# A two-block transformer kernel: the first block's output projection cut into two contraction halves, and the norm between the blocks done tile by tile

## What is computed

```python
sb_out = stick_breaking_attention(q, k, v)                  # 512 columns
sg_out = chunked_spatial_gating(u, vg, ...)                 # 512 columns
mixed = concatenate([rmsnorm(sb_out, sb_out_norm_g), rmsnorm(sg_out, sg_out_norm_g)])
h = h + mixed @ w_out
h = h + hierarchical_moe(rmsnorm(h, ffn_norm_g), ...)
x = rmsnorm(h, final_norm_g)                                # end of the first block
z = rms_norm(x, g_mix) @ w_in + b_in                        # start of the second block
```

## Time and profile before

| | us |
|---|---|
| median of three runs | 1077.96 (1077.39 to 1079.14) |
| profiled execution, time | 1080.09 |
| profiled execution, span | 1078.6 |
| PE busy in the span | 896.8 (83%) |
| DVE busy | 526.9 (49%) |
| ACT busy | 344.6 (32%) |
| POOL busy | 133.4 (12%) |

### The profile page before, as it was taken

How to read it: one execution, slowest core, us unless ns; L and a number is a source line. 1 busy time by engine, 2 the same in 40 slices (tenths; PEclk the granted TensorE clock), 3 DMA queues, 4 the chain that set the end, 5 groups by cost and what they waited for, 6 DMA issues and landing times.

```text
span 1078.6 us, 18062 instructions
## 1 busy us (share of the span) xinstructions
PE 896.8 (83%) x7891; PEld 724.1 (67%) x7891; DVE 526.9 (49%) x845; ACT 344.6 (32%) x463; POOL 133.4 (12%) x67
## 2 busy tenths in 40 slices
PE   8998988966475746475565899999999989999997
PEld 8987875533243424242342599689999989988986
DVE  4644554222131212112021769999997857635542
ACT  5624221100000001000000734557756446443531
POOL 1032400000000000000001288603210000000000
PEclk9998999888787868778688899999999999999999
DMA  9870748999999999999999645325568444546420
GB/s 343 260 300 2 300 168 371 426 426 427 426 428 428 428 428 430 428 428 430 428 428 420 198 162 191 117 93 171 168 211 283 173 170 166 207 157 218 173 78 39
DMA packets 86727, 299.98 MB, mean 278 GB/s; under 512 B 12381, under 2 KB 50701, under 8 KB 74253
## 3 DMA queue, kind: packets, MB, share of 16 engines
q1 hardware_dynamic: 86525, 299.13, 70.7%
q10 hardware_dynamic: 144, 0.00, 0.0%
HBM read 298.07 MB, written 1.05 MB: 277 GB/s over the span
## 4 chain that ended last, share of the span: by engine, by line
PE 52%; DMA 29%; DVE 14%; ACT 2%; issue 2%; SPq 1%; DVEq 0%
DMA mem<-in_w_up 25%; PE PS L1772 12%; PE PS L1773 12%; PE PS L1774 12%; PE PS L1954 8%; DVE PS L1547 6%; PE PS L1967 3%; DMA mem<-in_w_down 3%; DMA mem<-in_w_in 1%; DVE PS L1572 1%; PE PS L1940 1%; DMA mem<-in_w 1%; PE PS L1980 1%; PE PS L1746 1%; DVE PS L1568 1%
## 5 line engine op out<-in xcount | busy, mean ns | idle before, releaser
L1954 PE MATMUL PS<-mem 128*32 128x256 f32 x2048 | 156.6, 473 | 136.0 <-DMA mem<-in_w_up 135.4
L1954 PEld LDWEIGHTS PS<-mem 128*32 128x32 f32 x2048 | 83.6, 136 | 210.6 <-issue 184.6
L1774 PE MATMUL PS<-HT_hi,ring_rest 128*128 128x256 f32 x752 | 212.8, 283 | 0.0
L1774 PEld LDWEIGHTS PS<-HT_hi,ring_rest 128*128 128x128 f32 x752 | 143.9, 191 | 0.0
L1328 DVE TENSOR_TENSOR mem<-mem,PS 128x128 f32<-128x128 f32 x32 | 12.1, 379 | 261.2 <-ACT mem L809 261.2
L1772 PE MATMUL PS<-HT_hi,z_hi 128*128 128x256 f32 x440 | 124.9, 284 | 2.3 <-DVE ring_rest L1522 2.3
L1773 PE MATMUL PS<-HT_rest,z_hi 128*128 128x256 f32 x440 | 124.5, 283 | 0.0
L653 POOL TENSOR_TENSOR ring_rest<-mem,z_hi 128x2048 fp32r<-128x2048 f32 x19 | 87.6, 4622 | 95.1 <-DVE ring_rest L1522 55.9
L1685 DVE TENSOR_TENSOR ring_rest<-mem,mlp_hi 128x4096 fp32r<-128x4096 f32 x16 | 70.8, 4424 | 57.7 <-ACT mlp_hi L1027 57.7
L809 ACT ACTIVATE mem<-PS 128x128 f32<-128x128 f32 x32 | 8.9, 278 | 272.3 <-PE PS L1954 272.3
L1547 DVE SCALAR_TENSOR_TENSOR PS<-mem,CAW,PS 128x256 f32<-128x256 f32 x232 | 91.3, 480 | 0.0
(11 more groups left out here) (357 smaller groups left out, 1817.7 us busy)
## 6 DMA issues: line engine op xcount, KB each, us to landing
mem<-in_w_gate SPq DMA_DIRECT2D x32, 2048.0 KB, 16.5
mem<-in_w_up SPq DMA_DIRECT2D x32, 2048.0 KB, 20.9
mem<-in_w_down SPq DMA_DIRECT2D x31, 2048.0 KB, 12.7
mem<-in_w SPq DMA_DIRECT2D x16, 2048.0 KB, 8.1
mem<-in_w_in SPq DMA_DIRECT2D x30, 1024.0 KB, 5.3
mem<-in_w_in SPq DMA_DIRECT2D x4, 2048.0 KB, 18.3
mem<-in_w_b_out SPq DMA_DIRECT2D x4, 1536.0 KB, 8.9
mem<-in_w_out SPq DMA_DIRECT2D x2, 2048.0 KB, 14.7
```

What stands on the lines that cost most here:

```text
L1774: ins = nc.tensor.matmul(dst, s_rest, m_hi, start=False, stop=stop and n == len(terms) - 1, skip_group_check=True)
L1954: ins = nc.tensor.matmul(PS[SLOTS * j:SLOTS * (j + 1), bank, 0:2 * F_STRIP].rearrange("p (w n) -> p w n", w=2), xg[:, k, :], w[:, :, k, F_ ...
```

## The change

w_out is read so that a contraction chunk holds rows of one half only: chunks 0 to 3 the attention's 512 rows, 4 to 7 the gated unit's. The norm, turning, gain and split are then done for the gated half first, within the last pair of heads, and for the attention's half after it. The product is done in two halves of the contraction, the gated one first, summed in PSUM. The factor of both norms comes from Ln and Exp with one correcting step on DVE in place of a root. The tables are turned among the spatial weights. GpSimd splits w_out's second block first, into slot 3; the down load of expert 1 goes behind the product. Between the blocks, the work on a tile starts when its own two sums are in; GpSimd's first split waits for the normed rows; the first two products go pass by pass together; the first block's output rows go behind `rest_half(1)`.

The diff, its changed counts, index helpers and small loads left out:

```diff
-                   for n, at in enumerate((4 * SLOT_FLOATS, 4 * SLOT_FLOATS + HALF_FLOATS, a0 + D, a0 + D + HALF_FLOATS))]
+                   for n, at in enumerate((4 * SLOT_FLOATS, 4 * SLOT_FLOATS + HALF_FLOATS, 3 * SLOT_FLOATS, 3 * SLOT_FLOATS + HALF_FLOATS))]
...
+                    for half in range(2):
+                        ks = slice(KC // 2 * half, KC // 2 * (half + 1))
+                        sp.dma_start(chunked(n % RING, BLOCK)[:, ks, :], w_out1[half][:, :, b * BLOCK:(b + 1) * BLOCK]).then_inc(loaded[n % RING], 16)
...
-            sp.wait_ge(*in1_used(7))
-            load_down(1, *first[2])
             sp.wait_ge(rows, rows_before["ffn"])
...
             load_down(0, *second[2])
+            load_down(1, *first[2])
...
-            for n in range(4):
+            for n in OUT1_SPLIT:
                 raw, rest = out1_half(n)
-                if n == 2:
-                    pool.wait_ge(av_done, PAIRS)
-                    pool.wait_ge(hT_rest_ready, split_count("mix", 3))
...
             pool.wait_ge(z_hi_ready, 1)
+            pool.wait_ge(rows, rows_before["mix2"] + TT)
...
+            def mix_factor(col, rows_, *ready):
+                for tt in range(TT):
+                    act.wait_ge(*ready[tt])
+                    add_squares(rows_[tt], col + tt, square[:, 0:SB])
+                link(nc.scalar.activation(rstd[:, col:col + TT], ss[:, col:col + TT], ACT.Ln, scale=1.0 / SB, bias=eps[:, :]))
+                nc.scalar.activation(rstd[:, col:col + TT], rstd[:, col:col + TT], ACT.Exp, scale=-0.5).then_inc(rms_ready, 1)
...
             for pair in range(PAIRS):
                 if pair + 1 < PAIRS:
                     att_log(pair + 1)
+                else:
+                    mix_factor(6, [so[:, tt, :] for tt in range(TT)], (so_ready, 1), (so_ready, 2))
                 att_weights(pair)
-            act.preload_act_table_set(SQRT_SET)
...
+            split_hT("mix", range(TT))
+            mix_factor(4, [PS[:, 2 + tt, :] for tt in range(TT)], (av_done, PAIRS), (av_done, PAIRS))
+            split_hT("mix", range(TT, 2 * TT))
...
             gating(0)
+            gating(1)
             att_masked(2)
             att_softplus(3)
-            gating(1)
+            mix_rows("mix gated", 1, 6, [so[:, tt, :] for tt in range(TT)])
             att_masked(3)
...
+            apply_gain("mix", G_MIX, range(TT))
+            rest_hT("mix", range(TT))
+            mix_rows("mix", 0, 4, [PS[:, 2 + tt, :] for tt in range(TT)])
+            apply_gain("mix", G_MIX, range(TT, 2 * TT))
+            rest_hT("mix", range(TT, 2 * TT))
...
+            for tt in range(TT):
+                for n in (2 * tt, 2 * tt + 1):
+                    add_part(PACKS - 1, n)
+                    if n == 2:
+                        square_terms(0)
                 nc.vector.tensor_tensor(HG[:, tt, :], X[:, tt, :], g_first[:, :], ALU.mult).then_inc(gained, 1)
...
-            inverse_rms("first", 10, TT)
-            for tt in range(TT):
-                nc.vector.tensor_scalar(X[:, tt, :], HG[:, tt, :], rstd[:, 10 + tt:11 + tt], None, ALU.mult)
...
             rest_half(1)
+            inverse_rms("first", 10, TT)
+            for tt in range(TT):
+                nc.vector.tensor_scalar(X[:, tt, :], HG[:, tt, :], rstd[:, 10 + tt:11 + tt], None, ALU.mult)
             conv_a(0)
...
+            def out1_product(n, half):
+                pe.wait_ge(out1_rest_ready, OUT1_SPLIT.index(n) + 1)
+                for tt in range(TT):
+                    terms = rows_times(tt, out1_hi[n][:, :, :], out1_half(n)[1])[KC // 2 * half:KC // 2 * (half + 1)]
+                    ins = three_passes(out1_place(n, tt), terms, half == 1 and n % 2 == 0, half == 0)
...
+                if pair == PAIRS - 1:
+                    turn_mix(1, 0)
                 weighted_values(pair - 1)
             weighted_values(PAIRS - 1)
-            keep_busy(7, 4)
-            turn_rows("mix")
-            keep_busy(1, 3)
-            pe.wait_ge(hT_rest_ready, split_count("mix", 3))
...
+            pe.wait_ge(hT_rest_ready, split_count("mix", TT - 1))
+            out1_product(0, 1)
+            out1_product(1, 1)
+            turn_mix(0, TT)
+            out1_product(2, 1)
+            out1_product(3, 1)
+            pe.wait_ge(hT_rest_ready, split_count("mix", 2 * TT - 1))
             for n in range(4):
+                out1_product(n, 0)
...
+            def first_pair(hi, rest):
...
-                        if isinstance(r, int) and (r, h, i) == (0, 0, 0):
-                            first_times_hT(PS[:, 0, 0:T], hi, rest, slice(0, P), "mix2", z_rest_ready, 1).then_inc(z_ps, 1)
+                        if isinstance(r, int) and (r, h) == (0, 0):
+                            if i == 1:
+                                first_pair(hi, rest)
```

More of the change, by code:

```diff
@@ L296, in build @@
         norms = ["attn", "mix", "ffn", "mix2", "mlp2"]
-        rms_ready, rms_order = sem("rms_ready"), ("attn", "vg", "mix", "ffn", "mix2", "mix2 second", "first", "mlp2", "last")
+        rms_ready, rms_order = sem("rms_ready"), ("attn", "vg", "mix gated", "mix", "ffn", "mix2", "mix2 second", "first", "mlp2", "last")
         rows, rows_before = sem("rows"), {"attn": 0, "mix": TT, "ffn": 3 * TT, "mix2": 4 * TT, "mlp2": 5 * TT}
@@ L417, in late_used, with out1_count, out1_place @@
             return (f_ps, 16 * half + 4 * (b + 1)) if b < 4 else (w2_used, 4 * half + b - 3)
-        def pre_count(n):
-            return 16 * (n // RING + 1)
+        def out1_count(n):
+            return 16 * (n // RING + 2)
+        MIX_QUARTERS = [(tt, slice(KC // 2 * half, KC // 2 * (half + 1))) for half in (1, 0) for tt in range(TT)]
+        OUT1_SPLIT = (2, 3, 0, 1)
+        def out1_place(n, tt):
+            return PS[:, (0 if n < 2 else 6) + tt, (n % 2) * HALF:(n % 2 + 1) * HALF]
         def in1_used(n):
@@ L712, in split_hT @@
                 for n in quarters:
-                    tt, ks = n // 2, slice(4 * (n % 2), 4 * (n % 2) + 4)
+                    tt, ks = MIX_QUARTERS[n] if name == "mix" else (n // 2, slice(4 * (n % 2), 4 * (n % 2) + 4))
                     act.wait_ge(hT_ready, hT_count(name, n))
@@ L1498, in _, with square_terms @@
             collect(e + PACK - 1, PACK - 1)
-            add_pack(PACKS - 1)
-            for tt in range(TT):
+            def square_terms(tt):
                 dve.wait_ge(first_squares, tt + 1)
@@ L1885, in _, with turn_mix @@
             spatial_mixing(0)
+            def turn_mix(half, n0):
+                for tt in range(TT):
+                    pe.wait_ge(rows, TT + n0 + tt + 1)
+                    if n0 > 0:
+                        pe.wait_ge(hT_ready, hT_count("mix", n0 - TT + tt))
+                    for k in range(KC // 2):
+                        ins = nc.tensor.transpose(PS[:, 4 + tt, k * P:(k + 1) * P], HN[:, tt, KC // 2 * half + k, :], ident[:, :])
+                    ins.then_inc(turned, 1)
+            def out1_product(n, half):
+                pe.wait_ge(out1_rest_ready, OUT1_SPLIT.index(n) + 1)
+                for tt in range(TT):
+                    terms = rows_times(tt, out1_hi[n][:, :, :], out1_half(n)[1])[KC // 2 * half:KC // 2 * (half + 1)]
+                    ins = three_passes(out1_place(n, tt), terms, half == 1 and n % 2 == 0, half == 0)
+                    if half == 0:
+                        ins.then_inc(out1_ps, 1)
             for pair in range(1, PAIRS):
```

121 lines of the change are left out of this document (67 added, 54 removed).

## The result

The changed kernel took 1069.65 us in the median (1068.80 to 1071.34) against 1077.81, a ratio of 0.9924 (95%: 0.9907 to 0.9941). The forecast was 1069.7 us. The profiled execution took 1071.34 us, 1069.6 of it span; that of before was 1078.6. The total was right.

The account below looks back on a forecast made before the run. The prediction took the path through attention and projection to the weight stream's restart, and the norm before the convolution, to bound the kernel. 5.4 + 2.9 = 8.3 us off the median 1077.96 gave 1069.7, range 1064.0 to 1074.5.

Parts of the forecast that it names:

- named signs of being wrong: TensorE waiting at turn_mix or the second half, clock low beyond 113, 4 us row scalings before the convolution, DMA idle after 160.
- First block: 5.4 forecast: Attention and projection by w_out: the product ends at 135.1 instead of 140.48, 5.4 us earlier.
- The mask of the last pair: In attention, VectorE's mask queued behind the gated half's rows, near 102.2 instead of 100.78: 1.4 us late.
- its 4 us at half clock (2.0): In the first block's projection, the product's first 4 us run at half clock, costing 2.0 us.
- Between the blocks: 2.9 forecast: Norm between the blocks: first matmul of the second block at 611.3 instead of 614.17, 2.9 us earlier.
- PE's stall for Pool's split: Between the blocks, TensorE waits after the pair's first pass for Pool's first split: 0 to 1.7 us, taken as 0.
- the output rows cost 0: First block's output rows, beside Pool's subtractions ahead of the convolution, delay it 0 to 1 us, taken as 0.
- the pair takes the 7.8 us it took before: Between the blocks, the second block's first pair of products keeps its 7.8 us, as the same 48 matmuls.
- Pool's port (2): Rival: attention pairs lose 1.6 us more and output rows cost the convolution 2.9; gain 3.8, 1074.2 us; chance 0.12.
- The clock's rival (1): Rival: the clock doesn't fall in attention; first block gains 10.8 us instead of 5.4, total 1064.3; chance 0.13.
- The hidden first part (3): Rival: late loads hide the first block's gain; 1076.0 us; chance 0.07 with what else ends within 0.2%.
- the low clock (4): Rival: without fillers the clock stays low in the projection; up to 1090.8 us, slower than before; chance 0.06.

Follow-up runs that it names:

- e8: The changed kernel with the gated half's norm taken out of attention, behind the last pair, keeping two contraction halves; 1077.23 us, ratio 1.0000 to the kernel before.
- e1: The kernel before with only the first block's edits of the change; 1070.92 us, ratio 0.9941 to the kernel before.
- e2: The kernel before with only the edits between the blocks; 1077.24 us, ratio 0.9987 to the kernel before.
- e9: The changed kernel with plain matmuls filling PE's gaps between the blocks; 1071.44 us, ratio 0.9938 to the kernel before.
- e10: The kernel before with only the first block's edits, plus plain matmuls filling PE's gaps between the blocks; 1072.83 us, ratio 0.9958 to the kernel before.
- e4: The changed kernel with 14 plain matmuls in each of PE's two gaps inside attention; 1068.21 us, ratio 0.9914 to the kernel before.
- e3: The changed kernel with the two output rows put ahead of rest_half(1), where Pool stands idle; 1069.60 us, ratio 0.9929 to the kernel before.
- e6: The changed kernel with Pool's split of the first low part between the blocks put back ahead of the rows; 1072.12 us, ratio 0.9950 to the kernel before.
- e5: The changed kernel with the high parts of two halves of w_out made by ScalarE instead of Pool; 1067.32 us, ratio 0.9907 to the kernel before.

## Why the forecast came out right

**Structure.** The steps that were named happened: the product behind the last weighted values, nothing waiting in it, the stream's restart at 158.11 (forecast 158.5), Pool behind the rows, gained rows at 1.23 us, the product between the blocks 3.4 us sooner after the sums (forecast 2.9). e8 shows that without the overlap with attention the gain of the first block is gone, as the sum said. One of the named signs of being wrong came too: row scalings of over 4 us in front of the convolution (5.1 each).

**First block: 5.4 forecast, 6.8 in the trace of after (B; up to 9.1 in the six kernels with this attention), 6.4 by e1's ratio (3.8 to 8.8).** Terms were mis-sized with opposite signs. The weighted values end 4.1 us later than before (A) in place of 3.2. The last pair's key sums began at 101.9 (the 1.0 of the later start taken off) in place of 99.0: the third pair lost 1.4 at the port, not 0.8, and the clock fell in both gaps, not behind one, which made the key sums and scores from 92.65 to 97.7 take twice their time, 2.4 us more. Some 2 us of this came back behind them. The mask of the last pair was not late, as VectorE scaled the rows while PE summed the keys, and the last 24 small matmuls took 2.8 us at full clock (108.0 to 110.8) where 5 at half clock were forecast. The product was then 2.3 us shorter: its 4 us at half clock (2.0) did not come. Both terms rested on the inference that only dense matmuls bring the clock back, and it was wrong: at 107.9 the clock was back while PE ran eight turns. In e8 the half clock in the product does come.

**Between the blocks: 2.9 forecast; 0.8 and 1.0 at the convolution in traces of like clock, 0.6 to 2.2 by medians and ratios (e2; after against e1; e9 against e10), each with 2 us of noise or more, so that the size rests on the traces.** The lead at the first matmul was sized well. Three steps failed behind it. PE's stall for Pool's split, bounded at 0 to 1.7 and taken as 0, cost 0.4 in the trace of after and 1.0 in e9. That the output rows cost 0 had been bounded at 0 to 1; they cost 0.5 in the trace of after and 1.4 in e9. And "the pair takes the 7.8 us it took before" took the half clock in the trace of before as fixed; it was one draw of something that varies. The 3.1 us between the two profiled executions hold some 2 us that are this clock's and no gain of the change. The transfer and ScalarE's work between the pair and the convolution, which the forecast left out, took 8.2 us before and 8.0 after from SP's request on, so leaving them out cost nothing.

So 5.4 + 2.9 = 8.3 met 8.2 by luck: 1.0 to 1.4 us too little in one place (e1's ratio, after's trace) met 1 to 2 us too much in the other. Of the rivals, Pool's port (2) was at work at both its places, for 0.6 us more than taken in attention and 0.5 to 1.4 at the rows, less than half of the 4.5 it was priced at. The clock's rival (1) is e4: 2.1 to 2.8 us at B, not the 5.4 it was priced at, and part of it given back. The hidden first part (3) and the low clock (4) did not come.

## What to carry to other kernels

Before a difference of a few us between two traces is read as a gain, compare the granted clock over the same stretch in both; where it differs, cut the traces at marks and ask whether the rest agrees. An engine moved into a gap can slow another beside it: here VectorE's multiplies with two SBUF inputs and its row scalings were up to seven times faster where Pool was idle, and the order that counts is that of the operation the next engine waits for. Splitting the product by contraction paid here with the first half's inputs made beside other work; without that (e8) its earlier start was lost again. And a load or a cast between two stages can carry the path: read what the waiting engine waits for.

## What the hardware showed that was not expected

A scaling of 128x1024 from SBUF by a column took 0.75 us with Pool idle (e3) and 5.1 beside Pool's 4.6 to 4.8 us subtractions (after), a factor of seven; the same kind of scaling with a strided result took 1.4 us without Pool (after) and 2.1 beside it (e6). The Trainium skill, SBUF — State Buffer, section "Who interferes with whom", says that tensor_scalar can enter a two-port mode, and that of it and a Pool instruction the one that comes second is then blocked for the whole of the other; the 5.1 us agree. The multiplies with two SBUF inputs took 0.76 us for two without Pool and up to 2.70 (e4) beside Pool's pieces of 0.6 to 1.5 us, with 1.17 (e6) to 2.07 (e9) for the same two of the first pair in kernels with the same attention.

The granted clock fell to 1.2 GHz (0.50 of 2.4) in or behind gaps of 2.8 and 3.15 us on PE inside attention, and stayed there for 3 to 7 us in kernels with the same attention code, and for about 3 or 10 us in kernels with the same code between the blocks. The length of the gap alone doesn't decide it: the clock fell in one of 1.37 us (e5, where the key sums at 90.42 took 1.22 us) and not in or behind one of 1.36 in the kernel before (1.00 from 88 to 94 us):

```profile
90.44 0.70 PE L1846 MATMUL PS<-mem,masks 128*128 128x256 f32 x2 [1.36 <-DVE mem L1168]
```

Runs of the kernel before lay between 1073.4 and 1084.6 us.
